# Five feed-forward layers: rounded input and remainder moved side by side as 512 columns, halves added on VectorE

## The reference, cut to what matters

```python
def sq_relu_mlp(h, w1, w2):                   # sub-layers 1 and 3, width 4096
    return jnp.square(jax.nn.relu(h @ w1)) @ w2
def swiglu(x, w13, w2):                       # sub-layers 4, 6, 7, 9, width 2816
    gate, up = jnp.split(x @ w13, 2, axis=-1)
    return (jax.nn.silu(gate) * up) @ w2
```

## Time and profile before

| | us |
|---|---|
| median of three runs | 2263.32 (2262.86 to 2265.74) |
| span of the profiled execution | 2263.8 |
| TensorE busy | 2168.8 (96%) |
| VectorE busy | 1559.0 (69%) |
| ScalarE busy | 1133.0 (50%) |
| GpSimd busy | 352.8 (16%) |

### The profile page before, as it was taken

The page is one execution under the profiler, slowest core; times in us unless marked ns, Lnnn a source line. Parts: engine busy times, 40 slices in busy tenths (PEclk is TensorE's granted clock), DMA queues, the critical chain, the costliest instruction groups (busy, mean ns, idle before and its releaser), DMA issues.

```text
span 2263.8 us, 36177 instructions
## 1 busy us (share of the span) xinstructions
PE 2168.8 (96%) x15272; PEld 1997.2 (88%) x15272; DVE 1559.0 (69%) x1871; ACT 1133.0 (50%) x1500; POOL 352.8 (16%) x306
## 2 busy tenths in 40 slices
PE   4889999999999999999999999999999999999998
PEld 4668998887899899999899899999999988998997
DVE  6888897698755754569865774465456996757545
ACT  2344444796544443456664453344345767445342
POOL 2112324331110210030021140022003001112000
PEclk9899999999999999999999999999999999999999
DMA  9749894444365455665442465546566554235552
GB/s 358 240 143 333 300 329 152 119 115 126 133 215 191 157 198 187 166 190 150 122 118 70 149 205 183 181 149 220 185 182 168 154 136 112 94 124 183 194 189 93
DMA packets 304982, 396.96 MB, mean 175 GB/s; under 512 B 48032, under 2 KB 263706, under 8 KB 304821
## 3 DMA queue, kind: packets, MB, share of 16 engines
q1 hardware_dynamic: 285440, 336.75, 46.5%
q0 software_dynamic: 18496, 57.59, 8.1%
q10 hardware_dynamic: 884, 0.30, 0.1%
HBM read 393.53 MB, written 1.07 MB: 174 GB/s over the span
## 4 chain that ended last, share of the span: by engine, by line
PE 74%; DVE 15%; ACT 5%; issue 3%; DMA 1%; POOL 0%; SPq 0%; DVEq 0%; ACTq 0%; POOLq 0%
PE tiles L522 15%; PE tiles L523 15%; PE tiles L524 15%; PE y_rows L522 7%; PE y_rows L523 7%; PE y_rows L524 7%; DVE weights_lo L1439 4%; PE tiles L935 2%; ACT weights_hi L1053 2%; DVE ada_acc L1487 2%; DMA ada_ring<-in_ada_w_dram 1%; ACT xt L1090 1%; PE tiles L653 1%; PE tiles L629 1%; DVE rnn_gates L1769 1%
## 5 line engine op out<-in xcount | busy, mean ns | idle before, releaser
L1439 DVE TENSOR_TENSOR weights_lo<-weights_raw,weights_hi 128x2048 fp32r<-128x2048 f32 (+2 forms) x316 | 765.5, 2431 | 433.2 <-ACT weights_hi L1053 432.5
L522 PE MATMUL tiles<-xt_hi,weights_hi 128*128 128x256 f32 (+1 forms) x3200 | 911.6, 285 | 16.1 <-ACT xt L1090 7.0
L523 PE MATMUL tiles<-xt_lo,weights_hi 128*128 128x256 f32 (+1 forms) x3200 | 905.8, 283 | 0.0
L524 PE MATMUL tiles<-xt_hi,weights_lo 128*128 128x256 f32 (+1 forms) x3200 | 905.8, 283 | 0.0
L1053 ACT ACTIVATE weights_hi<-weights_raw 128x2048 fp32r<-128x2048 f32 (+2 forms) x316 | 592.3, 1878 | 218.0 <-PE y_rows L524 165.7
L522 PEld LDWEIGHTS tiles<-xt_hi,weights_hi 128*128 128x128 f32 (+1 forms) x3200 | 607.2, 190 | 31.9 <-issue 24.6
L523 PEld LDWEIGHTS tiles<-xt_lo,weights_hi 128*128 128x128 f32 (+1 forms) x3200 | 607.5, 190 | 2.7
L524 PEld LDWEIGHTS tiles<-xt_hi,weights_lo 128*128 128x128 f32 (+1 forms) x3200 | 607.4, 190 | 0.0
L522 PE MATMUL y_rows<-weights_hi,hid_hi 128*128 128x512 f32 x608 | 239.4, 394 | 0.5 <-DVE weights_lo L1439 0.5
L523 PE MATMUL y_rows<-weights_lo,hid_hi 128*128 128x512 f32 x608 | 237.8, 391 | 0.0
L524 PE MATMUL y_rows<-weights_hi,hid_lo 128*128 128x512 f32 x608 | 237.4, 390 | 0.0
(11 more groups left out here) (367 smaller groups left out, 2767.4 us busy)
## 6 DMA issues: line engine op xcount, KB each, us to landing
weights_raw<-in_ffn_w_dram SPq DMA_DIRECT2D x132, 1024.0 KB, 5.0
weights_raw<-in_mlp_w_dram SPq DMA_DIRECT2D x64, 1024.0 KB, 6.1
weights_raw<-in_w_in_dram SPq DMA_DIRECT2D x52, 1024.0 KB, 5.2
ada_ring<-in_ada_w_dram POOLq DMA_DIRECT2D x76, 512.0 KB, 5.3
weights_raw<-in_rnn_w_in_dram SPq DMA_DIRECT2D x16, 768.0 KB, 4.8
weights_raw<-in_w_in_dram SPq DMA_DIRECT2D x32, 256.0 KB, 4.3
weights_raw<-in_w_branch_a_dram SPq DMA_DIRECT2D x32, 256.0 KB, 4.8
weights_raw<-in_w_branch_b_dram SPq DMA_DIRECT2D x8, 1024.0 KB, 5.2
```

The lines of the kernel that those rows point to most:

```text
L522: pe.matmul(o, a, c, start=first, stop=False)
L523: pe.matmul(o, a, d, start=False, stop=False)
L524: return pe.matmul(o, b, c, start=False, stop=last)
L1439: dve.tensor_tensor(slot_view(WLO, m, NSPL), slot_view(RAW, m, NRAW), slot_view(WHI, m, NSPL).bitcast(F32), ALU.subtract).then_inc(*inc("l ...
```

## The change: what it does

In layers 3, 4, 6, 7 and 9 the first weights go through `wide_slot`. `XH` and `XL` now lie side by side per chunk in one tile `XHL`. Per pair (group, k) there is one matmul of the rounded weights with 512 columns (256 of hi, 256 of lo) into a whole bank, and one of the weights' remainder with 256 columns of hi, into the second half of the bank. The bank holds one group of 128 features: its halves have to be added. A slot has two banks, 16 matmuls of 512 columns and 16 of 256.

VectorE adds the halves (`halves`): one TENSOR_REDUCE per bank, 128x512 out of PSUM to 128x256 in SBUF, over pairs of elements that lie 256 apart. In `ffn` this is done for g into `RB` and for u into `VB`; ScalarE applies Silu in place in SBUF once both g banks are reduced, VectorE multiplies SBUF by SBUF, ScalarE rounds. In layer 3 VectorE reduces into `RB`, then one operation makes max(x, 0) * x; ScalarE copies that to round it, and no longer does Relu and Square. Layer 1 stays as it was, and so do the mixers, but for the place of `XH` and `XL`.

```diff
--- before.py
+++ after.py
@@ -135,10 +135,9 @@
         gbc_at = pos["at"]
         GB = put("ln_gb_rows", [P, 2, D])
         XS = put("x_scaled", [P, NT, D])
-        XH = put("xt_hi", [P, KC, S], F32R, at=pos["at"])
         act1 = pos["at"]
-        pos["at"] += 8 * KB
-        XL = put("xt_lo", [P, KC, S], F32R)
+        XHL = put("xt_hi_lo", [P, KC, 2, S], F32R)
+        XH, XL = XHL[:, :, 0, :], XHL[:, :, 1, :]
         act2 = pos["at"]
         OH = put("ot_hi", [P, KC, S], F32R)
         OL = put("ot_lo", [P, KC, S], F32R)
@@ -540,6 +539,19 @@
                               k == 0 and (j == 0 or not ready), k == nk - 1 and (j == nt - 1 or not ready))
                 ins.then_inc(*inc("tile_done", label))
 
+            def wide_slot(label, ready=None):
+
+                n, wh, wl = open_slot(label)
+                banks = [topen(label + (j,), "D") for j in range(2)]
+                order = [(j, k) for k in range(KC) for j in range(2)] if ready else [(j, k) for j in range(2) for k in range(KC)]
+                for j, k in order:
+                    if ready:
+                        ready(k)
+                    pe.matmul(banks[j], wh[:, k, j * P:(j + 1) * P], XHL[:, k, :, :].rearrange("p a b -> p (a b)"), start=k == 0, stop=False)
+                    ins = pe.matmul(banks[j][:, S:2 * S], wl[:, k, j * P:(j + 1) * P], XH[:, k, :], start=False, stop=k == KC - 1)
+                    if k == KC - 1:
+                        ins.then_inc(*inc("tile_done", label + (j,) if j == 0 else label))
+
             def v_slot(label, xh, xl, ready=None):
 
                 n, wh, wl = open_slot(label)
@@ -749,7 +761,10 @@
                 n = FF1 // 256
                 for i in range(n + 1):
                     if i < n:
-                        cols_slot((s, "w1", i), XH, XL, "A", ready=xready(s) if i == 0 else None)
+                        if s == 1:
+                            cols_slot((s, "w1", i), XH, XL, "A", ready=xready(s) if i == 0 else None)
+                        else:
+                            wide_slot((s, "w1", i), ready=xready(s) if i == 0 else None)
                         if i == (4 if s == 1 else 0):
                             gate_rows(s)
                     if s == 1 and i in (2, 4, 6, 8, 11, 13, 16):
@@ -784,8 +799,8 @@
                 n = FF2 // 256
                 for i in range(n + 1):
                     if i < n:
-                        cols_slot((s, "g", i), XH, XL, "A", ready=xready(s) if i == 0 else None)
-                        cols_slot((s, "u", i), XH, XL, "D")
+                        wide_slot((s, "g", i), ready=xready(s) if i == 0 else None)
+                        wide_slot((s, "u", i))
                     if i > 0:
                         hidden_rows(s, i - 1, n)
 
@@ -1157,12 +1172,16 @@
                 for i in range(n + 1):
                     if i < n:
                         step((s, "w1", i))
-                        bank = tile((s, "w1", i))
-                        if i >= 2:
-                            act.wait_ge(*past("hid_ready", (s, i - 2)))
-                        evac((s, "w1", i), RB[:, i % 2, :], ACT.Relu, bank)
-                        act.wait_ge(*past("free_A", (s, "w1", i)))
-                        hi_hidden(s, i, ACT.Square, RB)
+                        if s == 1:
+                            bank = tile((s, "w1", i))
+                            if i >= 2:
+                                act.wait_ge(*past("hid_ready", (s, i - 2)))
+                            evac((s, "w1", i), RB[:, i % 2, :], ACT.Relu, bank)
+                            act.wait_ge(*past("free_A", (s, "w1", i)))
+                            hi_hidden(s, i, ACT.Square, RB)
+                        else:
+                            act.wait_ge(*past("hid_v", (s, i)))
+                            hi_hidden(s, i, ACT.Copy, VB)
                         if i == (4 if s == 1 else 0):
                             gate_rows(s)
                     if s == 1 and i == 3:
@@ -1180,12 +1199,10 @@
                 for i in range(n + 1):
                     if i < n:
                         step((s, "g", i))
-                        bank = tile((s, "g", i))
-                        if i >= 2:
-                            act.wait_ge(*past("hid_ready", (s, i - 2)))
-                        evac((s, "g", i), RB[:, i % 2, :], ACT.Silu, bank)
+                        act.wait_ge(*past("free_D", (s, "g", i, 1)))
+                        act.activation(RB[:, i % 2, :], RB[:, i % 2, :], ACT.Silu).then_inc(*inc("free_A", (s, "g", i)))
                         step((s, "u", i))
-                        act.wait_ge(*past("free_D", (s, "u", i)))
+                        act.wait_ge(*past("hid_v", (s, i)))
                         hi_hidden(s, i, ACT.Copy, VB)
                     if i > 0:
                         step((s, "w2", i - 1))
@@ -1659,6 +1676,13 @@
                 if s + 1 < n_sub:
                     prep(s + 1)
 
+            def halves(label, dst):
+                for j in range(2):
+                    tile(label + (j,) if j == 0 else label)
+                    bank = TB[:, known.get(("tile", label + (j,)), 0) % NTB, :]
+                    dve.tensor_reduce(dst[:, j * S:(j + 1) * S], bank.rearrange("p (a b) -> p b a", a=2), AX.X, ALU.add).then_inc(*inc("free_D", label + (j,)))
+                dve.wait_ge(*past("free_D", label + (1,)))
+
             def lo_hidden(s, i):
                 dve.wait_ge(*past("hh_ready", (s, i)))
                 dve.tensor_tensor(HL[:, i % 2, :], VB[:, i % 2, :], HH[:, i % 2, :].bitcast(F32), ALU.subtract).then_inc(*inc("hid_ready", (s, i)))
@@ -1694,8 +1718,12 @@
                 for i in range(n + 1):
                     if i < n:
                         step((s, "w1", i))
-                        dve.wait_ge(*past("free_A", (s, "w1", i)))
-                        dve.tensor_tensor(VB[:, i % 2, :], RB[:, i % 2, :], RB[:, i % 2, :], ALU.mult).then_inc(*inc("hid_v", (s, i)))
+                        if s == 1:
+                            dve.wait_ge(*past("free_A", (s, "w1", i)))
+                            dve.tensor_tensor(VB[:, i % 2, :], RB[:, i % 2, :], RB[:, i % 2, :], ALU.mult).then_inc(*inc("hid_v", (s, i)))
+                        else:
+                            halves((s, "w1", i), RB[:, i % 2, :])
+                            dve.scalar_tensor_tensor(VB[:, i % 2, :], RB[:, i % 2, :], 0.0, RB[:, i % 2, :], ALU.max, ALU.mult).then_inc(*inc("hid_v", (s, i)))
                         dve.wait_ge(*past("hid_v", (s, i)))
                         lo_hidden(s, i)
                     if s == 1 and i in (2, 4, 6, 8, 11, 13, 16):
@@ -1712,10 +1740,11 @@
                 for i in range(n + 1):
                     if i < n:
                         step((s, "g", i))
+                        halves((s, "g", i), RB[:, i % 2, :])
                         step((s, "u", i))
-                        bank = tile((s, "u", i))
+                        halves((s, "u", i), VB[:, i % 2, :])
                         dve.wait_ge(*past("free_A", (s, "g", i)))
-                        dve.tensor_tensor(VB[:, i % 2, :], RB[:, i % 2, :], bank, ALU.mult).then_inc(*inc("free_D", (s, "u", i)))
+                        dve.tensor_tensor(VB[:, i % 2, :], RB[:, i % 2, :], VB[:, i % 2, :], ALU.mult).then_inc(*inc("hid_v", (s, i)))
                         lo_hidden(s, i)
                     if i > 0:
                         step((s, "w2", i - 1))
```

## The result

The changed kernel takes 2273.49 us, the median of four runs (2269.91 to 2274.47), beside 2264.09 for the kernel before on the same chip: a ratio of 1.0039 with a 95% interval of 1.0027 to 1.0051. A second set of five runs gave 2273.03 and 1.0040 (1.0026 to 1.0054). So it is slower by some 9 us, above the 0.2% that the prediction took as the limit of what can be told. The forecast was 2265.5, with "no change" as the likeliest outcome (0.41, against 0.35 for slower). The time lies outside the forecast's own range, 2261 to 2271, and inside the wider one for 8 in 10, 2249 to 2280; rival 2 had 2272 to 2279.

What follows compares the result with a forecast made beforehand. TensorE was taken to bound the changed layers. Losses of 17.75 us at starts and ends against gains of 15.9 us gave net +1.8, forecast 2265.5 us, own range 2261 to 2271, 8 in 10 within 2249 to 2280.

Steps and rivals of the forecast that it cites:

- rival 2: Slower: a pair gains only 0.003 to 0.007 us while the losses of 17.75 stay, 2272 to 2279 us; chance 0.14.
- What bounds the kernel: Layers 3, 4, 6, 7, 9: TensorE bounds; in the middle it still does after the change, with 0.9 us to spare.
- the loop of VectorE and ScalarE: Middle iterations: reductions, product, roundings, remainders and Silu alternate between two engines, some 15.7 us against TensorE's 16.59.
- TensorE's part: Each pair falls from 0.3597 to 0.3478 us, 0.192 us less per slot, 20.0 us at most over 104 slots.
- low end: Smallest gain per pair considered, 0.007 us instead of 0.012; it would add 8.5 us to the sum.
- the losses of 17.75 us: Lost time at starts and ends of layers 3, 4, 6, 7 and 9, summed.
- VectorE's added work: Two reductions of 512 elements out of PSUM per slot, 0.69 us each, bounds 0.60 and 1.37.
- The start: Layers 4, 6, 7, 9: the loop starts late without slack, so TensorE begins u2 2.9 us late.
- The ends: Later norm chain and transposes: 1.3 us in layers 4, 6, 7; 0.9 in layer 9; 0.8 in layer 3.
- Layer 3: Second slot 0.55 us late, 15 slots gain 0.192 each, end 0.8 later; about 1.5 us shorter.
- The sum: Losses 17.75 us less gains that count 15.9: net +1.8 us, written as 2265.5.

Runs made afterwards that it cites:

- e3: The changed kernel with every reduction done twice; 2361.36 us.
- e1: The changed kernel with each group's 8 matmuls of 512 columns first, then its 8 of 256, except in a layer's first slot; 2266.74 us.
- e9: The changed kernel with only iterations 0 to 2 of each changed layer as before the change, the end in the new form; 2262.16 us.
- e7: The changed kernel with iterations 0 to 2 and the last of each changed layer as before, the new form in the middle only; 2258.22 us.
- e12: The changed kernel run again with nothing altered; 2273.03 us, ratio 1.0040 to the kernel before.
- e4: The changed kernel with GpSimd's four scaling operations in layers 4, 6, 7 and 9 moved from the layer's start to iterations 1 to 4; 2262.49 us.
- e5: The kernel before the change with GpSimd's four scaling operations in layers 4, 6, 7 and 9 moved later in the same way; 2261.60 us.
- e11: The changed kernel with only the new side-by-side place of the activations, every slot used as before the change; 2264.09 us.
- e2: The changed kernel with the matmul of the weights' remainder also moving all 512 columns; 2423.46 us.

## Why the prediction was right or wrong

**What bounds the kernel: right.** The middle stayed with TensorE, and the loop of VectorE and ScalarE did not decide there. The prediction had it at 15.7 us; 15.0 follows from e3. Two reductions take 1.27 or 1.28 and not 1.38, which is 0.2 of the difference; the rest was not taken apart.

**TensorE's part: the term that failed.** The prediction says "It becomes one of 512 and one of 256, 0.2279 + 0.1199 = 0.3478", taken from stretches in which each size stands alone. Alternating they take 0.353: the gain is 0.0069 us a pair, not 0.012, and 0.110 a slot, not 0.192. The prediction had named 0.007 as its low end, from the 0.23 us starts among the first 512s behind 256s, but held the equal fixed part of 13 ns at both sizes against it. (Its own rows give 13.2 ns at 256 columns and 14.6 at 512, so the part was not quite equal.) It priced the difference at 1.3 us per ns, so 6.6 us; e1, which undoes the order, is shorter than after by 1.12, 1.24, 1.39, 1.37 and 1.44 us in the five layers, 6.6 together. The alternation also made seven rows stretches of a long layer 0.03 us longer, which no term covered: 0.2 us per long layer. This is rival 2's mechanism at the upper edge of its 0.003 to 0.007; the slot of 5.65 lies between the forecast's 5.56 and rival 2's 5.7. But rival 2 let the losses of 17.75 us stay, and they came out near 15. That the median fell into its 2272 to 2279 is in part luck: the changed layers give 2263.3 + 6.6 = 2270, and the rest stands outside of them.

By the Trainium skill's rule for an isolated gap (TensorE: Matmul & The Clock Gate, Back-to-back issue gap) a pair would save 2.5 ns; with the forecast's losses that is an estimate of some 14 us slower. Measured were 6.9 alternating and 11.6 grouped: neither is that figure, though the rule pointed to the right side.

**VectorE's added work: right.** 0.683 against 0.69. Product 0.692 against 0.69. The Silu was taken at 0.60 and is 0.632, which costs 0.03 per iteration on a loop with slack.

**The start: right in mechanism, 0.7 us too large.** Forecast were 2.9 us at u2. Layer 4's u2 starts at 807.45; shifted by 766.33 - 764.15 = 2.18 for what came before the layer, the old kernel's would start at 805.28: 2.17 late. Of the waits, TensorE lost 1.00 to the bank for u1, as worked out; then none at w2 where 0.7 was put, 0.24 at g2 (0.7) and 0.80 at u2 (1.4). The chain was faster than summed: with the same shift, the remainders for w2, g2 and u2 ended 0.4, 0.5 and 0.8 earlier than worked out. From the fourth iteration on no wait follows, as forecast.

**The ends: right in mechanism, smaller.** In layer 4 it is 10.68 us from the first matmul behind u10 (947.41) to the transposes (958.09), before 9.62: 1.06 for the forecast's 1.3. Net of the last slots' own gain (0.2, in layer 3 0.1), e9 against e7, it is 0.9 in layers 4, 6 and 7, 0.67 in layer 9 (forecast, not net: 0.9) and 0.54 in layer 3 (0.8). The wait inside the last rows is 0.53.

**Layer 3: the gain that was forecast is not there.** "About 1.5 shorter" came out at 0.0. Its 15 slots gain 1.7 and not 2.88, and the end costs 0.65 for 0.8. Its second slot waited more than the 0.55 put down; shifted as above, it starts 1.1 late, and waits for the bank:

```profile
588.94 0.47 PE L550 MATMUL tiles<-xt_hi_lo,weights_hi 128*128 128x512 f32 x1 [1.00 <-DVE hid_act L1683]
```

1.1 + 0.65 - 1.7 comes to the 0.0 of the table, within rounding.

**The sum again with measured sizes**, layer 4: 2.17 late at u2, less 17 x 0.110 = 1.87, plus 0.23 for seven rows stretches of 5.50 or 5.51 in place of 5.47, plus 1.06 for the end: 1.59, which is what the table shows. The other long layers are 1.57 to 1.79 longer. The forecast had 2.9 - 3.26 + 1.3 = 0.9. So two errors partly cancelled: the gain was sized 1.6 us too large per layer with its rows, the losses 1.0 too large. Over the layers that makes 6.6 in place of 1.8.

**Small slips in the sums, none of which moves the forecast.** The prediction compares the span of 2263.8 with the median of 2263.3. In this study a span is 1.7 to 1.9 us shorter than the time of the same execution (after: 2272.6 and 2274.47), so the profiled execution was some 2.4 us above the median, not 0.5. With 0.003 us a pair rival 2 gives 2277, not 2279.

**Not covered:** 2 to 3 us of the median outside the changed layers. Over the fifteen runs of the kernel before in the last set the time falls by 0.8 us per 0.001 of mean granted clock (0.989 to 0.993), and e12's five runs lie in the same range of clock, so this does not explain the surplus. One pattern of the record speaks for a real effect. In the four kernels that have the new form from a layer's first slot on (after, e12, e1, e4) the medians exceed before's by 1.9 to 2.8 us more than the changed layers add up to; in the six others (e5, e7 to e11) it is -0.5 to 1.3. And of the thirteen profiled executions only four show the fall near 186 us, all with the new form at the start: after, e2, e3 and e4. How a form used from layer 3 on could reach layer 1 no run shows, so a cause in the change stays open.

## What to carry to other kernels

Price an instruction by a row in which it has the neighbours it will have: two sizes measured in stretches of their own did not give the sum when they alternated, and the gain was little more than half as large. A form that wins in the steady state can lose at a layer's start and end, where the helper engines have no slack: use it only where they have some, and move the work of a third engine away from the tight place first.

## What was not expected of the hardware

- A 512-column matmul between 256-column ones held TensorE for 0.235 us, among 512s 0.2267 to 0.228; the 256s stayed at 0.117 to 0.120. The first seven to ten 512s behind two alternating slots are slow too (0.24, 0.24, 0.23), which makes that stretch 5.50 instead of 5.47; behind a single one, in layer 3, it took 5.47. The granted clock was at its full level in layers 3 and 4.
- It is not fixed to the order: in after, the pairs from 770.84 to 775.70 (14 pairs, 4.86 us) and those of the slots after the waits at 789.24 and 807.45 took 0.347, like grouped ones; the other 19 slots of layer 4 took 0.353. In e4 the first four slots of that layer all ran at 0.347, without a wait. Two states of the same sequence, then, and alternation alone does not bring the slower one; but from the fourth iteration on every slot looked at was in it. What sets the state is open.
- A reduction of 512 elements out of PSUM over pairs that lie 1 KB apart took 0.683 us, no more than the contiguous one of 0.686 in the earlier trace rows, and was not held up by GpSimd.
- When GpSimd's operations stand beside VectorE's remainders, moving them out of the layer's start gave back 2.4 to 2.7 us in the kernel whose loop is tight there, and 0.53 in the one with slack.
